# First mixer: the last head pair's sample states ahead of its numerators, and eight weight thirds held back behind them; second mixer: page values and read-backs of transposes placed one step later

## The reference, cut to what matters

```python
# first mixer, per chunk of 128 tokens (for the samples: one chunk of 4 tokens)
s   = einsum('bhtd,bhsd->bhts', qi, ki) * exp(log_d - m_t)
num = w_inter * einsum('bhtd,bhde->bhte', qi, c) + einsum('bhts,bhse->bhte', s, vi)
den = w_inter * einsum('bhtd,bhd->bht', qi, n) + sum(s)
h   = num / maximum(abs(den), exp(-m_t))
c_new = decay * c + einsum('bhs,bhsd,bhse->bhde', w_k, ki, vi)      # the new states
h = sigmoid(o) * rmsnorm(h, g_head);  mix = h @ w_out
# second mixer: A[t,s] = beta_ts * prod_{s<j<t}(1 - beta_tj), s < t
z = q @ k.T / 8 + bias;  log1mb = where(mask, log_sigmoid(-z), 0)
a = exp(where(mask, z + cumsum(log1mb, reverse=True), -inf));  out = a @ v
```

## Time and profile before

| what | us |
|---|---|
| median of three runs | 2983.94 (2976.22 to 2984.82) |
| profiled execution | 2977.9, its span 2976.1 |
| PE busy | 2847.8 (96%) |
| DVE, ACT, POOL busy | 1303.7 (44%), 819.4 (28%), 731.6 (25%) |
| first mixer | to about 463 |
| projection and MLP | 463 to 1323 |
| second mixer | 1323 to about 2111 |
| projection, MLP, output norm | 2111 to 2976 |

### The profile page before, as it was taken

One profiled execution on the slowest core, in us unless ns is written; L12 is line 12 of the kernel. 1 busy time (PEld: TensorE's weight loads), 2 busy tenths in 40 slices (PEclk: granted clock), 3 DMA queues, 4 the chain that ended last, 5 costly groups with the idle time before them and its releaser, 6 DMA issues. The chain is left out here.

```text
span 2976.1 us, 49009 instructions
## 1 busy us (share of the span) xinstructions
PE 2847.8 (96%) x19713; PEld 2609.5 (88%) x19713; DVE 1303.7 (44%) x1851; ACT 819.4 (28%) x1675; POOL 731.6 (25%) x449
## 2 busy tenths in 40 slices
PE   7999998999999999999999999998899999999998
PEld 6988887999999999986777677665799999999997
DVE  6323345433333333355556655565543333333334
ACT  5221123201110011125555655556320111001112
POOL 3222102223232232322112111210222323223231
PEclk9999998999999999999999999999899999999999
DMA  5575524222323223234343443434311111111112
GB/s 164 187 148 187 100 30 102 92 86 86 98 85 99 85 89 94 86 103 120 113 121 107 115 128 108 121 101 114 123 50 43 44 49 42 49 42 47 45 43 79
DMA packets 361448, 277.23 MB, mean 93 GB/s; under 512 B 31379, under 2 KB 352915, under 8 KB 359251
## 3 DMA queue, kind: packets, MB, share of 16 engines
q1 hardware_dynamic: 340074, 261.97, 30.3%
q10 hardware_dynamic: 21224, 13.15, 2.3%
HBM read 251.06 MB, written 91.11 MB: 115 GB/s over the span
## 5 line engine op out<-in xcount | busy, mean ns | idle before, releaser
L162 POOL CAST w_hi<-w_raw 128x1024 fp32r<-128x1024 f32 x193 | 206.2, 1068 | 1606.8 <-PE bank L214 904.6
L212 PE MATMUL bank<-p_u_hi,w_hi 128*128 128x352 f32 x1536 | 496.6, 323 | 7.2 <-DVE p_u_lo L2166 5.8
L212 PE MATMUL bank<-x_hi,w_hi 128*128 128x352 f32 x1536 | 496.0, 323 | 1.7 <-PEq L2256 1.7
L213 PE MATMUL bank<-p_u_lo,w_hi 128*128 128x352 f32 x1536 | 495.7, 323 | 0.0
L214 PE MATMUL bank<-p_u_hi,w_lo 128*128 128x352 f32 x1536 | 495.5, 323 | 0.0
L214 PE MATMUL bank<-x_hi,w_lo 128*128 128x352 f32 x1536 | 493.8, 321 | 0.0
L213 PE MATMUL bank<-x_lo,w_hi 128*128 128x352 f32 x1536 | 493.2, 321 | 0.0
L164 POOL TENSOR_TENSOR w_lo<-w_raw,w_hi 128x1024 fp32r<-128x1024 f32 x193 | 468.2, 2426 | 15.5
L2116 ACT ACTIVATE p_u_hi<-p_relu 128x352 fp32r<-128x352 f32 x192 | 95.7, 499 | 1207.0 <-DVE p_relu L2163 1207.0
L2172 DVE TENSOR_TENSOR h<-bank,h 128x352 f32<-128x352 f32 x384 | 198.6, 522 | 467.1 <-PE bank L214 467.1
L2166 DVE TENSOR_TENSOR p_u_lo<-p_relu_sq,p_u_hi 128x352 fp32r<-128x352 f32 x192 | 229.1, 1193 | 182.7 <-ACT p_relu_sq L2117 182.7
(11 more groups left out here) (271 smaller groups left out, 4426.6 us busy)
## 6 DMA issues: line engine op xcount, KB each, us to landing
k_pages<-in_cache_k SPq DMA_DIRECT2D x64, 512.0 KB, 5.9
w_raw<-in_w_up SPq DMA_DIRECT2D x64, 512.0 KB, 4.0
v_pages<-in_cache_v SPq DMA_DIRECT2D x64, 512.0 KB, 4.7
w_raw<-in_w_down SPq DMA_DIRECT2D x64, 512.0 KB, 3.4
p_pages<-k_pages SPq DMA_DIRECT2D x256, 128.0 KB, 2.4
p_pages<-v_pages SPq DMA_DIRECT2D x256, 128.0 KB, 2.4
w_raw<-in_w_in_a SPq DMA_DIRECT2D x25, 512.0 KB, 4.1
h_spill<-h SPq DMA_DIRECT2D x16, 528.0 KB, 5.2
```

The costliest lines, as they stand in the source:

```text
L162: pool.tensor_copy(m.whi[slot][:, :], m.wraw[slot][:, :]).then_inc(w.hi, 1)
L212: pe.matmul(bank[:, 0:TW], wh, xh, start=(k == 0), stop=False)
L213: pe.matmul(bank[:, 0:TW], wh, xl, start=False, stop=False)
```

## The change

In the first mixer's last pair the three "dcs" steps stand each behind its "dc" step instead of at the end. So that the numerators can still read the old sample states, the new ones go to the other buffer, Cs[0], and DVE waits until that buffer's earlier contents are stored. The "v" steps of the pair have no third behind them any more, and with the shift eight thirds stand behind the last numerators. On DVE, the denominators, sums and scaling of the last pair are put between the reads of the three tiles that these thirds make, instead of behind them all. On ACT the last pair's sigmoids come behind inverse_rms, with a table load of their own, and each of the two waits for its own panel.

In the second mixer follow(y) comes one turn later (behind the turn after next), and one is left over into the next slot, behind its z. Value quarters 0 and 1 stand together behind the first turn, quarter 2 stays behind the fourth, and quarter 3 with the products of the new rows moves into the slot after (2 or 6), behind its second turn; ACT's read of the result moves with it.

```diff
-    FILL_LAST = {"u": 1, "k": 1, "v": 1, "wsp": 1, "out": 0, "scores": 1, "dc": 1, "dcs": 0, "num": 1}
+    FILL_LAST = {"u": 1, "k": 1, "v": 0, "wsp": 1, "out": 0, "scores": 1, "dc": 1, "dcs": 0, "num": 1}
...
-        return out + [("num", p, x) for x in range(3)] + [("dcs", p, x) for x in range(3)]
+        sample = [("dcs", p, x) for x in range(3)]
+        if p == HP - 1:
+            out = [y for x in out for y in ((x, sample[x[2]]) if x[0] == "dc" else (x,))]
+            sample = []
+        return out + [("num", p, x) for x in range(3)] + sample
...
+        def Cs_out(p):
+
+            return Cs[(p + (p == HP - 1)) % 2]
...
             def output_gates(p):
-                act.wait_ge(w.tile_free[0], taken(p, 5))
                 for h2 in range(2):
+                    act.wait_ge(w.tile_free[0], taken(p, 4 + h2))
                     act.activation(m.h[:, 2 * p + h2, :], m.h[:, 2 * p + h2, :], ACT.Sigmoid).then_inc(o_ready, 1)
 
             def squares(p):
-                if p != HP - 2:
+                if p < HP - 2:
                     output_gates(p)
...
-                    if x == ("v", HP - 1, (0, 1)):
+                    if x == ("v", HP - 1, (0, 2)):
                         output_gates(HP - 2)
+                    if i == 1 and p == HP:
+                        output_gates(HP - 1)
...
-                if x == 0:
+                if x == 0 and p < HP - 1:
 
                     dve.wait_ge(num_in, 3 * p + 3)
+                elif x == 0:
+
+                    dve.wait_ge(state_out, 64 * p)
+                    dve.wait_ge(state_in, 32 * p + 32)
                 for i, b in enumerate(range(*TRIO_S[x])):
-                    last = dve.scalar_tensor_tensor(out=Cs[p % 2][:, b, :], in0=Cs[p % 2][:, b, :], scalar=decb[:, p, NC + b:NC + b + 1],
+                    last = dve.scalar_tensor_tensor(out=Cs_out(p)[:, b, :], in0=Cs[p % 2][:, b, :], scalar=decb[:, p, NC + b:NC + b + 1],
...
-                    for t, part in fill:
-                        if part == len(THIRDS) - 1:
-                            read_out(tau_of(p, t))
+                    done = [tau_of(p, t) for t, part in fill if part == len(THIRDS) - 1]
+                    if p == HP - 1 and i == len(PLANS[p]) - 1:
+                        assert len(done) == 3
+                        denominators(p)
+                        read_out(done[0])
+                        sums(p)
+                        read_out(done[1])
+                        scale_heads(p)
+                        read_out(done[2])
+                    else:
+                        for tau in done:
+                            read_out(tau)
...
-    VALUES_AFTER = {0: [0], 1: [1], 3: [2]}
+    VALUES_AFTER = {0: [0, 1], 3: [2]}
+    LAST_VALUES_AT, LAST_AFTER = {2: 0, 6: 1}, 1
...
+            def settle(left):
+
+                while len(pending) > left:
+                    follow(pending.pop(0))
+
...
                 if tiles:
                     z(p, n, 0)
-                before = None
+                settle(0)
                 for i, y in enumerate(turns_of(slot)):
                     turn(y)
+                    settle(1)
+                    pending.append(y)
...
-                    if before is not None:
-                        follow(before)
-                    before = y
                     for x in VALUES_AFTER.get(i, ()):
                         if x < len(quarters):
                             values(*quarters[x])
+                    if i == LAST_AFTER:
+                        for q, g in at(LAST_VALUES_AT, slot):
+                            values(q, g, QUARTERS - 1)
...
-                if before is not None:
-                    follow(before)
+                settle(1 if 0 <= slot < SLOTS * PAIRS - 1 else 0)
```

More of the change, by code:

```diff
@@ L1298, in sums @@
                 step(dve.tensor_tensor(den2[:, :, :], den[:, :, :], den[:, :, :], ALU.mult))
+            def sums(p):
                 for h2 in range(2):
@@ L1322, in _ @@
             for p in range(HP + 1):
-                if p:
+                if 0 < p < HP:
+                    denominators(p - 1)
                     sums(p - 1)
-                if p == HP:
-                    scale_heads(p - 1)
                 for i, (x, fill) in enumerate(PLANS[p]):
@@ L1709, in values @@
                     last.then_inc(pvs_done, 1)
+            pending = []
+            def settle(left):
+                while len(pending) > left:
+                    follow(pending.pop(0))
             def turns(slot, fill, d):
                 p, n = divmod(slot, SLOTS)
-                quarters = [(q, g, x) for q, g in at(VALUES_AT, slot) for x in range(QUARTERS)]
+                quarters = [(q, g, x) for q, g in at(VALUES_AT, slot) for x in range(QUARTERS - 1)]
                 tiles = 0 <= p < PAIRS
@@ L1735, in turns @@
                     d, fill = d + 1, fill - 1
-                if before is not None:
-                    follow(before)
+                settle(1 if 0 <= slot < SLOTS * PAIRS - 1 else 0)
                 if len(turns_of(slot)) < 2 and lower:
                     z(p, n, 1)
+                assert len(turns_of(slot)) > LAST_AFTER or not at(LAST_VALUES_AT, slot)
                 placed = sum(len(x) for i, x in VALUES_AFTER.items() if i < len(turns_of(slot)))
@@ L1864, in _ @@
                         gates(p, n, *due.pop(0))
-                    if i and turns[i - 1][0] == "page" and turns[i - 1][2][2] == SG - 1:
-                        gates_sample(turns[i - 1][1], *turns[i - 1][2][:2])
+                    if i == LAST_AFTER + 1 - (turns[LAST_AFTER + 1:][:1] in [[("ys", q, g)] for q, g in at(LAST_VALUES_AT, slot)]):
+                        for q, g in at(LAST_VALUES_AT, slot):
+                            rows_sample(q, g)
+                    if i >= 2 and turns[i - 2][0] == "page" and turns[i - 2][2][2] == SG - 1:
+                        gates_sample(turns[i - 2][1], *turns[i - 2][2][:2])
                 if slot == EARLY:
@@ L1869, in _ @@
                     act.wait_ge(chain, 2)
-                if turns and turns[-1][0] == "page" and turns[-1][2][2] == SG - 1:
-                    gates_sample(turns[-1][1], *turns[-1][2][:2])
+                for y in turns[-2:]:
+                    if y[0] == "page" and y[2][2] == SG - 1:
+                        gates_sample(y[1], *y[2][:2])
                 for x, h2 in due:
                     gates(p, n, x, h2)
-                for q, g in at(VALUES_AT, slot):
-                    rows_sample(q, g)
         @block.vector
```

6 lines of the change are left out of this document (3 added, 3 removed).

## The result

The change made the kernel faster: 2947.19 us (median of 4 runs, 2942.16 to 2951.66) against 2981.93 us of before on the same chip; ratio 0.9885, 95% interval 0.9861 to 0.9910. The forecast was 2952 (2935 to 2973). The profiled execution took 2944.42 us against 2977.9 before, 33.5 us less where 28.2 were forecast.

| stage | before | after | change | forecast |
|---|---|---|---|---|
| start to barrier behind the first mixer | 463.60 | 458.58 | -5.0 | -9.0 |
| barrier to the second mixer's start | 859.83 | 859.33 | -0.5 | 0 |
| second mixer, to the next block's first matmul | 792.09 | 764.58 | -27.5 | -19.2 |
| tail | 860.58 | 860.11 | -0.5 | 0 |

The account below looks back on a forecast made before the run. PE, busy for 96% of the span, was taken as the bound, so only its idle time counted. First mixer -9.0 and second mixer -19.2 made -28.2 us: 2977.9 to 2949.7, as a median 2952, range 2935 to 2973.

Parts of the forecast that it names:

- What bounds the kernel: Whole kernel: PE is busy for 96% of the span, so only time in which PE stands still can be won.
- The wait for scaled heads, and what is late next: First mixer's end: PE's 9.5 us wait nearly goes; POOL's splits end last, 7.1 us behind PE's last third; barrier -9.0 us.
- The sample states' 1.9 us: First mixer's last pair: PE's two waits for sample states, 1.9 us together, go.
- New waits at output turns, 1.2 us: First mixer's last pair: without "v" thirds PE waits for DVE to read the bank; 1.2 us, bounds 0 and 2.9.
- DVE's chain from the numerators: First mixer's end: from numerators at 437.3, denominators take 3.2 us, scaling 2.63; heads scaled at 447.4 and 448.7.
- Behind the barrier, no credit for the clock: Dense work after the first mixer: half clock for its first 4.3 us stays despite a shorter sparse stretch; 0 us credited.
- Waits in the second mixer, 2.35 us a pair: Seven pairs: 0.87 for value pages, 0.2 in slot 2, 0.7 for three 0.24 us waits, 0.57 in slot 6; 16.5 us.
- The rest of the second mixer: Outside the seven pairs: only the last pair's page waits, 2.7 us, counted; second mixer -19.2 us in all.
- rival 1: Second mixer: every turn needs the copy two turns back, so only page waits go, some 4 us; 2965 to 2971; chance 0.20.
- rival 2: First mixer: less cover at six "v" steps exposes 8.6 us, so it gives nothing; 2959, median 2962; chance 0.07.
- rival 3: Second mixer: ACT's copies wait for later PE products and gates behind them slip by 0.58 us; 3014 us; chance 0.04.
- rival 4: Second mixer: ACT starts earlier, so waits of 0.62, 0.82 and 0.98 us go too, 17 us more; 2935; chance 0.09.

Follow-up runs that it names:

- e6: New kernel with POOL's two weight splits at the first mixer's end in the other order, the last tile's last; 2947.10 us, ratio 0.9879 to the old kernel.
- e3: New kernel with the value quarters put back in their old places, so the second mixer keeps only the later follow; 2971.71 us, ratio 0.9955 to the old kernel.
- e7: New kernel with one more third in each of slots 2 and 3 of the second mixer, taken from slots 6 and 7; 2937.58 us, ratio 0.9848 to old.
- e1: New kernel with the old kernel's second mixer, so only the first mixer is changed; 2977.36 us, ratio 0.9979 to the old kernel.
- e4: New kernel with follow one turn late as before, so in the second mixer only the value quarters moved; 2955.16 us, ratio 0.9899 to the old kernel.
- e9: New kernel with the old follow and quarter 3 back at its slot's end; in the second mixer only value quarter 1 moved; 2963.91 us, ratio 0.9941 to old.
- e2: New kernel with the old kernel's first mixer, so only the second mixer is changed; 2955.48 us, ratio 0.9904 to the old kernel.
- e5: New kernel with one third put back behind the second head's first value transposes in the first mixer's last pair; 2948.33 us, ratio 0.9877 to the old kernel.
- e10: New kernel with a third behind each "v" step of the first mixer's last pair again, two held back instead of eight; 2953.34 us, ratio 0.9899 to old.

## Why the prediction was right, and where it missed

The sign, the size and the range held: 33.5 us against 28.2 in the profiled execution. The two parts were off by 4.0 and 8.3 us to opposite sides, and most of the 8.3 is clock, which no step of the forecast counted; that the sum fits so well is in part luck. Step by step:

- *What bounds the kernel.* Right that PE does, but not that only time in which it stands still can be won: 21.6 us came out of its idle time and 11.9 out of its busy time, by the clock.
- *The wait for scaled heads, and what is late next.* Right as a mechanism. PE finds the heads ready when the thirds end, and POOL's splits are last, at 7.0 us behind the thirds (7.1); e6 shows it. The sample states' 1.9 us went.
- *New waits at output turns, 1.2 us.* This is the term of the first mixer that was mis-sized: ahead of the numerators they measured 2.95, in two waits, with none before; that is the bound of 2.9. I had taken the first to be one third of 1.44 us less the 0.84 us that DVE waited before, 0.6. But this is not PE's margin. These rows of before show it:

```profile
411.12 0.74 DVE L1319 SCALAR_TENSOR_TENSOR h<-bank,p_g_head,h 128x512 f32<-128x512 f32 x1
```

```profile
412.06 0.60 PE L832 MATMUL bank<-identity,p_numerator 128*128 128x128 f32 x4
```

DVE was done with the bank at 411.86 and PE's turn began at 412.06: a margin of 0.20 us. The rest of DVE's 0.84 is mostly the turn's own 0.60. So 1.44 - 0.20 = 1.24 us were due by the third alone. The rest is in DVE's chain ahead of that turn, 5.4 us of unbroken work from 403.45: inside it a copy of 128x32 takes 1.25 us where it took 0.18 before, 1.07 more; the section on the hardware tells why. Together 2.31, and 2.21 were measured. The second wait adds 0.74. Then came the half clock at 410 us, which was in no step. Its cost can be read off: from the matmul at 391 us to the barrier it is 66.7 us in after, e3 and e7, which have it, and 65.1 in e1, e4 and e9, which have the same first mixer without it, so 1.5 us. Together 3.3 us more than taken, and after was 0.5 us late at 391 already; the numerators came 3.7 late, and of the 9.0 us 5.0 were left (5.55 counted from 391, and 7.1 in e1).
- *DVE's chain from the numerators.* Scaling ended 9.7 us behind the numerators' end, where the forecast had 448.7 - 437.3 = 11.4: the denominators took 0.9 us instead of 3.2, since POOL's splits no longer lie beside them. The same mechanism as above, with the other sign; it stayed under cover of the thirds.
- *Behind the barrier, no credit for the clock.* Nearly right: half clock reached 3.1 us into the dense work (462.39 to 465.5) instead of 4.3 or a little more, and that stage was 0.5 us shorter.
- *Waits in the second mixer, 2.35 us a pair.* Right in the sum: 32.9 us fell to 16.5 over seven pairs, by 16.4 where 16.5 were forecast. In the parts: the value pages' 0.87, the three 0.24 and the 0.57 went, the 0.98 stayed, as forecast. In slot 2 I had 0.7 us come back by late key pages. They did not: the wait of 0.78 there ends with ACT's copy, not with a DMA, and is the 0.62 for page keys, a little longer. In its place stand 0.23 us at a page turn of slot 3 and 0.27 at z, which I had not seen. The two errors cancel.
- *The rest of the second mixer.* It became 27.5 us shorter, not 19.2. Idle time gave 18.0 of it, about as forecast (of the last pair's 2.7 us of page waits 1.2 went). The other 9.5 are busy time, a term that I had at nothing: the time at half clock fell from 36.0 to 19.5 us, and half of that difference is 8.2 us. But this is not a price of the change alone. e2, e5, e6 and e10 have after's second mixer and its pairs of 92.8 to 92.9 us, with 32 to 38 us at half clock and 770.2 to 773.5 us in all; after's 764.6 is the short one. And before's 792.1 is short too, beside the 798 or so that I estimate above as usual. What the medians support is e2's 29.3 us. Its idle time in the mixer is 46.6 us, 17.5 below before. The rest, some 12 us, would be clock, by an estimate from one trace of each: half clock that the old pairs get again and again (once in before, six times in e1) and the new ones don't. In them no page wait over 0.6 us is left, and slot 2 has one wait in place of two; the 0.23 and 0.98 us close together in slot 3 brought no half clock.
- *Rivals.* Both banks keep the pace (rival 1): false, e3's pairs without half clock give 1.0 us by the lag alone. First mixer gives nothing (rival 2): false, but its mechanism, exposed turns, took 1.75 us more than taken, and 1.5 came with it at half clock. Slower by ACT's queue (rival 3): not seen, in 1345 to 2010 us ACT has no wait for the products (L1713). ACT early enough that 0.62, 0.82 and 0.98 go (rival 4): not seen, 0.98 stayed, and slot 2 still has 0.78.

What stays open: why the place at 410 us drops to half clock in after, e3, e6 and e7 but not in e1, e4 and e9, where PE's wait ahead of it is the same 2.2 us (e5, with 0.8 us, hasn't it either, but by one execution that tells little). Nor is it settled why the two waits of slot 2 brought half clock three times in e1, once in e9 and not in before or e3, or why before's page waits of 1.34 and 1.45 us (at 1674 and 1865) passed without it.

## What to carry to other kernels

When a filler is taken from in front of a wait, count the whole unbroken chain of the other engine that the filler covered, from its start, and look what will run beside that chain at its new place; the time that the other engine stands idle is not the margin, since it waits through your own next step too. A short wait in a steady loop costs more than its length where PE drops to half clock behind it, as it did here behind seven of nine page waits of 1.3 us and more, so a page load with no slack is worth moving even if its wait reads under 1 us on average. One profiled execution of each kernel is not enough to price this; hold it against the medians. And spread filler by where PE waits: two thirds moved per pair gave 1.9 us a pair, beside 2.9 for the whole reordering.

## What the runs showed of the hardware

**DVE and POOL exclude each other on some operations.** The DVE copy L1254 (L1244 in before) takes 0.18 us in before and e10, where no POOL split lies beside it, and 1.25 us in after, from 403.45 to 404.70; POOL's split ends there at 402.26 + 2.40 = 404.66. e5 has 1.26 us likewise. In before the operation of 128x18 at L1298 took 1.92 us, from 449.94 to 451.86, under this POOL row of before, which ends at 451.83:

```profile
449.42 2.41 POOL L164 TENSOR_TENSOR w_lo<-w_raw,w_hi 128x1024 fp32r<-128x1024 f32 x1
```

In after it (L1312) takes 0.18 with no POOL work beside. The one at L1294 took 0.76 us instead of 0.20, and ends 0.04 us after POOL's cast before that split (448.30 + 1.04). In e10 both are hit in turn: DVE's first half of scaling (1.36 us from 450.93) holds POOL's split, 3.57 instead of 2.35 us, and the split, which ends at 454.51, holds DVE's second half, 3.52 instead of 1.35. Not every DVE operation is held: sums of 128x1024 (TENSOR_REDUCE) take 1.22 us beside a split (e10) and 1.21 to 1.22 without. The Trainium skill (SBUF — State Buffer, SBUF: two separate sides) says that the two share a pair of ports as an exclusive lock, held for a whole instruction, and that a DVE operation needs it in a two-port mode, or with two SBUF inputs if the POOL operation reads SBUF (these do); the trace agrees, to 0.04 us in the first two cases. I had read this effect, 2.3 us in the denominators (1.74 and 0.56), as the cost of the operations.

**Half clock in steady work.** A wait of 1.4 to 2.1 us for page values, in work in which PE is otherwise busy for 95%, was followed by 3.4 us at 1.2 GHz in seven places (before at 1482, three in e1, three in e3), each worth some 1.7 us by an estimate, half of 3.4; the place at 411 us in the first mixer measured 1.5. Two such waits, 1.34 and 1.45 us in before, were not followed by it. The two waits of 0.82 and 0.62 us in slot 2 were followed by it three times in e1 and once in e9 (at 1482), but in no pair of before or e3. It and the longer stretches at the mixer's start and in its last pair make the time of one kernel scatter: the same second mixer took 764.6 us in after, with 19.5 us at half clock, and 773.5 in e5, with 37.6. That the waits cause the drops was not tested by itself; they are what stands ahead of each in the steady pairs.
